# A fused two-block transformer kernel: scaling and turning the second token half behind the rms norms, and the order of the next stage's first chunk

## The reference, cut to what matters

```
x = x + forgetting_attention(rms_norm(x, g)) @ a_w_out        # "aw_out" is the last product
x = x + conv_ffn(rms_norm(x, ffn_g0), up0, ..., down0)        # "up0", "down0"
kv = rms_norm(x, kv_norm_g) @ w_kv                            # "wk" is the keys' half
q  = rms_norm(x, mix_g1) @ b_w_q
x = x + dilated_attention(q, kv) @ b_w_out                    # "bw_out"
x = x + conv_ffn(rms_norm(x, ffn_g1), up1, ..., down1)        # "up1", "down1"
return rms_norm(x, final_norm_g)

def rms_norm(x, g): return x * rsqrt(mean(x*x, axis=-1) + 1e-6) * g
def conv_ffn(h, w_up, conv_w, conv_b, w_down):
    a, gate = split(causal_conv3(h @ w_up) + conv_b)
    return (silu(gate) * a) @ w_down
```

## Time and profile before

| | |
|---|---|
| median of 3 runs | 1781.32 us (1780.11 to 1781.4) |
| the profiled execution, own time | 1781.06 us |
| its span, first to last instruction | 1779.8 us |
| mean granted TensorE clock | 0.998 of full |
| busy: PE, PEld, DVE, ACT, POOL | 1714.7, 1119.3, 790.1, 624.1, 121.0 us |
| DMA queue q1, mean over the span | 75.7% of 16 engines |

### The profile page before, as it was taken

How to read it: one execution, slowest core, us unless ns; L and a number is a source line. 1 busy time by engine, 2 the same in 40 slices (tenths; PEclk the granted TensorE clock), 3 DMA queues, 4 the chain that set the end, 5 groups by cost and what they waited for, 6 DMA issues and landing times.

```text
span 1779.8 us, 24004 instructions
## 1 busy us (share of the span) xinstructions
PE 1714.7 (96%) x10024; PEld 1119.3 (63%) x10024; DVE 790.1 (44%) x1510; ACT 624.1 (35%) x1197; POOL 121.0 (7%) x143
## 2 busy tenths in 40 slices
PE   9999999999989989999999889999999999999998
PEld 8974344433334974444343333887999898789986
DVE  6961111111103782111111012866888677668875
ACT  5541110000002661000000002666666564756664
POOL 0000000000000000000000000131111001401100
PEclk9999999999999999999999999999999999999999
DMA  9769999999999789999999999533555544335550
GB/s 389 310 230 357 402 429 427 428 428 427 426 425 419 285 322 367 429 428 429 428 428 426 425 426 419 182 123 137 182 181 188 189 166 146 138 129 175 184 189 24
DMA packets 55940, 544.90 MB, mean 306 GB/s; under 512 B 6288, under 2 KB 6288, under 8 KB 8336
## 3 DMA queue, kind: packets, MB, share of 16 engines
q1 hardware_dynamic: 55440, 542.14, 75.7%
q10 hardware_dynamic: 384, 1.13, 0.2%
HBM read 542.19 MB, written 1.05 MB: 305 GB/s over the span
## 4 chain that ended last, share of the span: by engine, by line
PE 68%; DMA 20%; DVE 7%; ACT 3%; issue 1%; POOL 1%; SPq 0%; DVEq 0%; ACTq 0%
PE PS L1144 23%; DMA ring<-in_w 20%; PE PS L410 12%; PE PS L412 11%; PE PS L411 11%; PE PS L1124 2%; DVE wl L393 2%; PE PS L1198 1%; PE PS L861 1%; PE PS L1160 1%; PE PS L620 1%; ACT wh L387 1%; PE PS L1212 1%; PE PS L1307 0%; DVE F L996 0%
## 5 line engine op out<-in xcount | busy, mean ns | idle before, releaser
L1144 PE MATMUL PS<-ring,F 128*64 128x512 f32 x2072 | 463.7, 597 | 28.0 <-DMA ring<-in_w 23.5
L393 DVE TENSOR_TENSOR wl<-ring,wh 128x512 fp32r<-128x512 f32 x504 | 363.1, 739 | 167.5 <-ACT wh L387 165.0
L387 ACT ACTIVATE wh<-ring 128x512 fp32r<-128x512 f32 x504 | 314.7, 631 | 271.7 <-PE PS L412 258.3
L1144 PEld LDWEIGHTS PS<-ring,F 128*64 128x64 f32 x2072 | 146.5, 137 | 323.0 <-issue 281.5
L410 PE MATMUL PS<-xh,wl 128*128 128x256 f32 x1168 | 336.5, 288 | 2.4 <-DVE wl L393 2.3
L411 PE MATMUL PS<-xl,wh 128*128 128x256 f32 x1168 | 330.3, 283 | 0.0
L412 PE MATMUL PS<-xh,wh 128*128 128x256 f32 x1168 | 330.3, 283 | 0.0
L410 PEld LDWEIGHTS PS<-xh,wl 128*128 128x128 f32 x1168 | 223.8, 192 | 5.6 <-DVE wl L393 2.7
L411 PEld LDWEIGHTS PS<-xl,wh 128*128 128x128 f32 x1168 | 223.9, 192 | 0.7
L412 PEld LDWEIGHTS PS<-xh,wh 128*128 128x128 f32 x1168 | 223.9, 192 | 0.0
L410 PE MATMUL PS<-wh,xl 128*128 128x512 f32 x352 | 142.5, 405 | 6.4 <-DVE xl L527 3.4
(11 more groups left out here) (393 smaller groups left out, 1885.5 us busy)
## 6 DMA issues: line engine op xcount, KB each, us to landing
ring<-in_w SPq DMA_DIRECT2D x100, 2048.0 KB, 25.6
ring<-in_w SPq DMA_DIRECT2D x65, 1024.0 KB, 11.6
ring<-in_ffn_up SPq DMA_DIRECT2D x44, 1024.0 KB, 4.9
early<-in_w SPq DMA_DIRECT2D x16, 2048.0 KB, 27.7
F<-in_w SPq DMA_DIRECT2D x16, 2048.0 KB, 28.9
ring<-in_ffn_down SPq DMA_DIRECT2D x22, 1024.0 KB, 4.8
F<-in_w SPq DMA_DIRECT2D x20, 1024.0 KB, 8.4
ZX<-in_w SPq DMA_DIRECT2D x8, 2048.0 KB, 29.1
```

What stands on the lines that cost most here:

```text
L387: act.e.activation(self.wh[:, p % NPIECE, :], self.piece_source(p), ACT.Copy).then_inc(*self.up("w_hi", p))
L393: dve.e.tensor_tensor(self.wl[:, p % NPIECE, :], self.piece_source(p), f32(self.wh[:, p % NPIECE, :]), ALU.subtract).then_inc(*self.up("w_ ...
L1144: t = pe.e.matmul(PS[64 * half:64 * half + 64, bank, :], lhs(k), weights[:, a:a + 512], start=(k == 0), stop=(k == 7))
```

## The change

It changes the three handovers. (1) The half-1 diagonal goes: DVE multiplies features 0 to 511 of X's half 1 by 1/rms and ACT features 512 to 1023, into Z; TensorE turns them with plain transposes (identity). Half 0 keeps the diagonal, but no longer waits for the last residual. (2) Pieces 0 and 2 of the next stage are split on ACT between the squares of the two halves, piece 1 behind the squares of half 1 and ahead of ACT's scaling; DVE splits piece 0 ahead of half 1's sum and pieces 2 and 1 behind its scaling. Piece 3 is split between tile pairs 1 and 2 of x. (3) Chunk 0 does both output tiles together: for k = 0..3 four matmuls on xh (two for each output tile), then the xl ones, then the same for k = 4..7; the two sums lie in two banks (0 and 1, in wk 0 and 3). Each rounded tile has its own signal. (4) In wk, the copy of chunk 0's keys becomes two copies, and chunk 3 waits for them. The loads and their order are as before.

```diff
+    def first_chunk(self, stage):
+        a, b = (0, 3) if stage == "kv" else (0, 1)
+        return self.PS[:, a:b + 1:b - a, 0:256]
+
+    def tensor_first_chunk(self, stage, p):
+        pe, out = self.pe, [self.first_chunk(stage)[:, j, :] for j in range(2)]
+        for half in range(2):
+            blocks = range(4 * half, 4 * half + 4)
+            for k in blocks:
+                a = slice(k % 4 * 128, k % 4 * 128 + 128)
+                pe.wait_ge(self.at("x_hi", stage, k // 2, k % 2))
+                for j in range(2):
+                    n = p + 2 * j + half
+                    h, l = self.weight(n)
+                    pe.wait_ge(self.at("w_lo", n))
+                    pe.e.matmul(out[j], l[:, a], self.xh[:, k, :], start=k == 0, stop=False)
+                    pe.e.matmul(out[j], h[:, a], self.xh[:, k, :], start=False, stop=False)
+            for k in blocks:
+                a = slice(k % 4 * 128, k % 4 * 128 + 128)
+                pe.wait_ge(self.at("x_lo", stage, k // 2))
+                for j in range(2):
+                    n = p + 2 * j + half
+                    t = pe.e.matmul(out[j], self.weight(n)[0][:, a], self.xl[:, k, :], start=False, stop=k == 7)
+                    if k % 4 == 3:
+                        t.then_inc(*self.up("w_used", n))
+    def vector_scaled(self, stage):
+        self.dve.wait_ge(self.at("rstd", (stage, 1)))
+        self.dve.e.tensor_scalar(self.Z[:, 1, 0:512], self.X[:, 1, 0:512], self.sm[:, 501:502], None, ALU.mult).then_inc(
+            *self.up("scaled", stage, 0))
+    def scalar_scaled(self, stage):
+        self.act.wait_ge(self.at("rstd", (stage, 1)))
+        self.act.e.activation(self.Z[:, 1, 512:1024], self.X[:, 1, 512:1024], ACT.Copy, scale=self.sm[:, 501:502]).then_inc(
+            *self.up("scaled", stage, 1))
     def vector_out_rms(self, stage, p, nk, following):
+        p1 = PIECES[following]
...
         self.vector_residual(stage, p, nk, 1, 1.0, self.X, halves=(1,))
+        self.vector_split(p1)
         self.vector_rms_sum(stage, 1)
-        self.vector_rms(stage, 1)
+        self.vector_scaled(stage)
+        self.vector_split(p1 + 2)
+        self.vector_split(p1 + 1)
+    def scalar_out_rms(self, stage, following):
+        p1 = PIECES[following]
+        self.scalar_rms(stage, stage, 0)
+        self.scalar_split(p1)
+        self.scalar_split(p1 + 2)
+        self.scalar_rms(stage, stage, 1)
+        self.scalar_split(p1 + 1)
+        self.scalar_scaled(stage)
+    def tensor_rms_features(self, stage, src_stage):
+        pe, PS, up, at = self.pe, self.PS, self.up, self.at
+        pe.wait_ge(at("diag", src_stage, 0))
+        for k in range(8):
+            pe.e.matmul(PS[:, 4 + k // 2, k % 2 * 256:k % 2 * 256 + 128], self.X[:, 0, k * 128:k * 128 + 128],
+                        self.Z[:, 0, 0:128], start=True, stop=True)
+        for k in range(8):
+            pe.wait_ge(at("scaled", src_stage, k // 4))
+            t = pe.e.transpose(PS[:, 4 + k // 2, k % 2 * 256 + 128:k % 2 * 256 + 256],
+                               self.Z[:, 1, k * 128:k * 128 + 128], self.ident[:, :])
+            if k % 2:
+                t.then_inc(*up("turned", stage, k // 2))
...
# at the head of ffn_scalar, ffn_vector (and alike in dilated_scalar, dilated_vector):
-        for n in range(2):
-            self.scalar_split(p + n)
         for q in range(4):
+            if q == 2:
+                self.scalar_split(p + 3)
             act.wait_ge(at("turned", stage, q))
             self.scalar_rms_split(stage, q, f"ffng{layer}", self.bank2(4 + q))
-        for n in (2, 3):
-            self.scalar_split(p + n)
...
# dilated_tensor:
         for c in range(6):
-            if c >= 4:
-                pe.wait_ge(self.dilated_k(c - 4))
-            for _ in self.tensor_features("kv", p + 4 * c, c % 4, c == 0):
+            if c == 0:
+                self.tensor_first_chunk("kv", p)
+                continue
+            if c >= 3:
+                pe.wait_ge(self.dilated_k(c - 4 if c > 3 else 0))
+            for _ in self.tensor_features("kv", p + 4 * c, c % 4):
```

More of the change, by code:

```diff
@@ L766, in scalar_rms_split @@
         for k in (2 * q, 2 * q + 1):
-            t = act.e.activation(xh[:, k, :], src[:, k % 2, :], ACT.Copy, scale=g[:, k:k + 1])
-        t.then_inc(*self.up("x_hi", stage, q))
+            act.e.activation(xh[:, k, :], src[:, k % 2, :], ACT.Copy, scale=g[:, k:k + 1]).then_inc(
+                *self.up("x_hi", stage, q, k % 2))
     def vector_rms_split(self, stage, q, gain, src):
@@ L2192, in forget_scalar @@
                                     at("w_used", PIECES["av1"] + 2 * q + 1))
-        for h in range(2):
-            self.scalar_rms("aw_out", "aw_out", h)
+        self.scalar_out_rms("aw_out", "up0")
     def forget_scalar_slot(self, s):
@@ L2228, in out_scalar @@
         if stage != "down1":
-            for h in range(2):
-                self.scalar_rms(stage, stage, h)
+            self.scalar_out_rms(stage, "wk")
             return
@@ L2256, in out_vector @@
         else:
-            self.vector_out_rms(stage, p, nk)
+            self.vector_out_rms(stage, p, nk, "wk")
     def forget_vector(self):
@@ L2324, in forget_vector @@
                 self.vector_split_x("aw_out", q, self.GT[:, 2 * q:2 * q + 2, :])
-        self.vector_out_rms("aw_out", PIECES["aw_out"], 8)
+        self.vector_out_rms("aw_out", PIECES["aw_out"], 8, "up0")
     def forget_vector_slot(self, s):
@@ L2383, in ffn_tensor @@
         stage, down = f"up{layer}", f"down{layer}"
-        self.tensor_to_features(stage, self.X, 4, [[at("diag", before, h)] for h in range(2)],
-                                [[at("resid", before, 1, 1)]] * 4, [self.Z[:, h, 0:128] for h in range(2)])
+        self.tensor_rms_features(stage, before)
         p = PIECES[stage]
         for n in range(22):
-            pe.wait_ge(at("taps", layer, n - 4) if n >= 4 else at("x_lo" if n else "x_hi", stage, n))
-            for _ in self.tensor_features(stage, p + 4 * n, self.ffn_bank(n), n == 0):
+            if n == 0:
+                self.tensor_first_chunk(stage, p)
+                continue
+            pe.wait_ge(at("taps", layer, n - 4) if n >= 4 else at("x_lo", stage, n))
+            for _ in self.tensor_features(stage, p + 4 * n, self.ffn_bank(n)):
                 pass
@@ L2464, in ffn_vector @@
         G, acc, th = self.ffn_views()
-        for n in range(2):
-            self.vector_split(p + n)
         for q in range(4):
+            if q == 2:
+                self.vector_split(p + 3)
             self.vector_rms_split(stage, q, f"ffng{layer}", self.bank2(4 + q))
-        for n in (2, 3):
-            self.vector_split(p + n)
         for n in range(22):
@@ L2645, in dilated_scalar @@
             self.scalar_split_before(p + n + NPIECE, p + 8)
-        for h in range(2):
-            self.scalar_rms("bw_out", "bw_out", h)
+        self.scalar_out_rms("bw_out", "up1")
     def dilated_scalar_slot(self, s):
@@ L2725, in dilated_vector @@
             self.vector_split_before(p + n + NPIECE, p + 8)
-        self.vector_out_rms("bw_out", p, 4)
+        self.vector_out_rms("bw_out", p, 4, "up1")
     def dilated_vector_slot(self, s):
```

25 lines of the change are left out of this document (14 added, 11 removed).

## The result

The changed kernel takes 1778.14 us (median of 22 runs, 1777.03 to 1779.51) against 1780.89 us for the kernel before (22 runs beside it): ratio 0.9984, 95% interval 0.9978 to 0.9990. That is 2.75 us less, 0.16%, with an interval of about 1.8 to 3.9 us; it is less than the 0.2% from which on I had called a difference measurable, yet the interval excludes 1, so the kernel is faster by a little. The forecast was 3.70 us less.

A forecast was written before the change was run, and what follows sets the result against it. TensorE was taken as the bound, busy 538 of 554 us. Gains of 1.45 us per handover, less 0.14 in two and 0.37 in up1, sum to 3.70: 1781.32 becomes 1777.6 us, range 1776.4 to 1779.3.

The forecast's parts named there:

- (a): Whole kernel: handover gains come as worked out, 1777.6 us, own range 1777.0 to 1778.7; chance 0.58.
- the start of the turning: Each handover, second half: first transpose at 1236.44 in the first handover, 0.04 us after VectorE's scaling ends.
- the earlier start of chunk 0: Each handover: chunk 0's first matmul starts 4.3 us after the last output matmul instead of 4.93, gaining 0.63 us.
- Splits early: Between the squares of the two halves: early weight splits cost 0 and leave the root unmoved, with 0.3 us cover.
- Scaling at 0.48 and 0.72: Second half of X: scaling 512 columns takes 0.48 us on DVE and 0.72 on ACT.
- Transposes: Second half's turning: 8 one-record transposes instead of 16 records; first pair turned at +0.44 us, rounding starts 0.04 later.
- Chunk 0 without a wait: Chunk 0 after each handover: 48 matmuls run without waits, 5.74 us plus 0.10 first gap, saving 0.82 us.
- p+5's stall of 0.14: Chunk 1's 13th matmul in up0 and wk: piece p+5's split comes 0.04 us late, plus 0.10 gap, 0.14 lost.
- Rival (b): Chunk 1: the stall on piece p+5 does not form, total 1777.3 us, or 1777.0 with up1's covered; chance 0.20.
- Up1 alone: Third handover: row-gains load delays piece p+4's split, so chunk 1 starts late; 0.27 + 0.10 = 0.37 us lost.
- Rival (c): Chunks 1 to 3: backlogged DVE splits hold up TensorE, giving back most of the gain; 1779.5 to 1781 us, chance 0.18.
- Rival (d): At the handovers: TensorE idles, then only transposes, so its clock falls and the kernel is slower, 1795 us; chance 0.04.

The follow-up runs named there:

- e1: Changed kernel with a separate signal for each engine's scaling of the second half instead of one shared counter: 1777.64 us, ratio 0.9981 to the kernel before.
- e9: Changed kernel with a third split (piece p+1) also placed between the squares of the two halves: 1778.27 us, ratio 0.9983 to the kernel before.
- e4: Changed kernel with the splits of pieces p and p+2 behind the second half's squares, VectorE's of p behind its sum: 1779.49 us, ratio 0.9990.
- e3: Changed kernel with chunk 0 in the old order, one output tile and then the other: 1783.04 us, ratio 1.0009 to the kernel before.
- e5: Changed kernel with chunk 0's last eight matmuls ordered by output tile, releasing piece p+1 three matmuls sooner: 1778.00 us, ratio 0.9982 to the kernel before.
- e6: Changed kernel with up1's load of the final norm's gains issued after piece p+7's split, not before p+4's: 1778.30 us, ratio 0.9983 to the kernel before.
- e7: Changed kernel with the edits of e8, e5 and e6 together: 1776.77 us, ratio 0.9976 to the kernel before.
- e8: Changed kernel with own signals as in e1, and VectorE's scaling in two instructions of 256 columns: 1777.12 us, ratio 0.9976 to the kernel before.
- a0: The changed kernel itself, unedited, run beside e7 on the same chip: 1778.78 us, ratio 0.9986 to the kernel before.

## Why the prediction was right or wrong

The time was inside the stated range, and the direction was right. The sum was 3.70 us; the traces show 2.85 to 2.93, the medians 2.75. Of faster by over 0.2% and within 0.2%, which I gave 0.50 and 0.46, the second came. Two things in this are luck. The time came nearer to the forecast (1778.14 against 1777.6) than the gain did, because the kernel before itself ran at 1780.89 beside it and not at the 1781.32 from which I had started. And the gain came out at the 2.7 that I had called (a)'s lower end, but neither of the two terms that I had priced for it, a slower scaling and slower transposes, occurred.

**The term that was mis-sized is the start of the turning, and with it the earlier start of chunk 0, 0.63 us a handover.** That start came 0.38 earlier instead. "First start 1236.44 (a release takes 0.04)" took the first transpose to wait for VectorE's half alone. It waited for both. Measured: 3.55 us behind the last output matmul instead of 3.30, and the whole error passes through to chunk 0, which starts at +4.55 instead of +4.30. e1 gave the missing wait back: 0.23 us a handover, 0.7 of the 0.77 us by which the sum was larger than the 2.93. It could have been read in the diff and the kernel without any trace: the step number of a shared counter is given in program order, and the order of ScalarE's and VectorE's lists was in the text.

Step by step:

- *Splits early, cost 0:* right; the root stands 2.74 to 2.75 us behind the last output matmul before and after. Cover 0.44 instead of 0.3 (e9). What they save is 0.55 a handover (e4).
- *Scaling at 0.48 and 0.72:* right, 0.49 and 0.72.
- *Transposes:* 8 records; first pair to rounding 1237.61 - 1237.14 = 0.47, as against 0.48. Right. (Rows 9 give 0.41 for the end of the second transpose, (0.55 - 0.273) / 2 ahead of that of the third, and not the 0.44 that I took; the difference is small beside the rest.)
- *Chunk 0 without a wait, 5.84 us:* right, 5.86; the alternation between banks costs nothing (L458 and L459 at 0.12 throughout), and e3 shows that without this part the other parts would have made the handovers longer than before.
- *p+5's stall of 0.14:* right, 0.15, and it is the chain that I named (e5). Rival (b), that it would not form, is refuted: the lateness was 0.05 us where 0.04 had been worked out. That so small a margin came out on the forecast side is partly luck, since other terms of the sum were off by more.
- *Up1 alone, 0.37:* 0.22 in the stretch and 0.10 in the gap behind, 0.32, and its cause is the wait and the issue (e6).
- *Rival (c), given back in later chunks:* refuted; 0.08 of 512 us apart from the named stalls, and 0.05 in e7.
- *Rival (d), the clock:* refuted. The granted clock is 1.00 in all three stretches, and TensorE's pause ahead of the transposes was 1.07 us, 1.0 forecast. Rows 12 had been thinner evidence than I made of them, for the pause ahead of their sixteen transposes was 0.35 us. The rule in the Trainium skill (TensorE: Matmul & The Clock Gate, Part 4) that transposes don't count as busy had no consequence here: eight of them behind such a pause did not lower the clock. What a longer row of transposes would do, no run here shows.

Open remains what the medians can't resolve: the steps of 0.2 to 0.7 us of e1, e5, e6 and e8 stand on traces, one for each kernel. Open is also how the 0.80 us inside chunk 0 divides between the new order and the moved splits.

## What to carry to other kernels

Where two engines count up one semaphore, the wait for "the first half" is a wait for a number, and which half has the lower number follows from the order of the program text; give each producer its own signal (e1). To number the half that is ready first lower would not be safe by itself: the count doesn't tell which engine made it, so a wait for 1 would also be passed when the other half came first. Where TensorE waits for operands that another engine delivers one by one, raise its work per delivered tile above the delivery time (here 0.48 us of matmuls against 0.36 us a tile). With the splits moved to suit it, this took 0.80 us out of chunk 0, and the earlier start gave 0.38. And such a reordering moves the release of buffers to its end: look for the next consumer of the release before it is late.

## What the runs showed of the hardware that I had not expected

- The part ahead of the first handover, the same instructions in every one of these kernels, came to its last output matmul between 1232.20 us (e6) and 1234.05 us (a0) over the traces, while each stretch of 10 us behind it repeated to 0.02 us. From that matmul to the end the two traces of the changed kernel take 543.81 us (1777.4 - 1233.59) and 543.75 (a0, 1777.8 - 1234.05), the kernel before 546.66. In these traces the scatter of the time is made up ahead of the first handover, and stretches tell edits apart that run times can't.
- A wait of TensorE that is late by hundredths costs 0.10 us more: the gap between the matmul that waited and the next is 0.22 instead of 0.12. Of the 0.62 us of small stalls in the changed kernel (0.15, 0.15 and 0.32), 0.30 is this.
